# A hybrid decoder trunk on one core: weight slabs split earlier at the stages' seams, and six more convolution taps on TensorE

## The chip, the cores and the metric

One core of one Trainium2 chip runs the whole kernel. The metric is the device time in microseconds, the median of the runs. Before the change it is 932.27 us (three runs, 932.22 to 932.45).

## The reference

Two layers on 256 tokens of width 1024, all in float32. Each layer is an FFN, a token mixer and another FFN, and a final RMSNorm ends the trunk:

```python
for i in range(2):
    x = x + 0.5 * swiglu_ffn(rms_norm(x, ffn1_norm[i]), ffn1_w_in[i], ffn1_w_out[i])
    xn = rms_norm(x, mix_norm[i])
    x = x + (pool_conv_mixer(xn, ...) if i == 0 else sgu_mixer(xn, ...))
    x = x + 0.5 * swiglu_ffn(rms_norm(x, ffn2_norm[i]), ffn2_w_in[i], ffn2_w_out[i])
out = rms_norm(x, final_norm)
```

An FFN has hidden width 2816: `(silu(gate) * up) @ w_out` with gate and up from one input matrix of 1024 x 5632. The even mixer projects to 512 pooling channels and 2 x 512 convolution channels. The first go through causal means over 2, 4, 8 and 16 tokens, a 128 x 128 matrix for each group and a scale. The others go through `a * sigmoid(gate)`, a causal depthwise convolution of 31 taps, LayerNorm over the 512 channels, and swish. One output matrix joins both. The odd mixer is a spatial gating unit: GELU, LayerNorm, a masked 128 x 128 matrix for each of 8 heads along the tokens, and an output matrix.

## The kernel before

Every product with weights is computed in three fp32r matmuls (`three`, L960): both operands are split into a high and a low part, and hi x hi, hi x lo and lo x hi are summed. Weights come from HBM in slabs of 128 x 2048 floats. SyncE loads each slab in two halves into a ring of RAW = 3 buffers (`load`, L231); a load waits until the low part of the slab three before it is done. ScalarE copies a slab to its high part `w_hi` (`split`, L444). VectorE subtracts to get the low part `w_lo` (`split`, L660). Both parts stand in a ring of RING = 6 slabs, and a split waits until TensorE has used the slab six before it. On each of the two engines `split_to(n)` splits all slabs up to n that are still to be split, at the place where it stands. An engine works strictly in the order of the program, so these places decide what stands ahead of what.

There are six stages: 0 is FFN, 1 the even mixer, 2 and 3 are FFNs, 4 is the odd mixer and 5 an FFN. `b` is the first slab of a stage. An FFN has 11 units. A unit uses two input slabs (the upper and lower half of the 1024 input rows) for 256 gate and 256 up channels. Token tile 0 is summed in PSUM bank `ga`, token tile 1 in `ub`, 24 matmuls each. ScalarE applies silu to the gate half of a bank (`gate_rows`), and VectorE multiplies by the up half (`product_rows`, L753), which frees the bank for the next unit. The product is transposed by TensorE (`turned`, L1061) in the middle of the next unit. ScalarE copies its high part (`hidden_hi`), VectorE subtracts the low part (`hidden_lo`, L761), and then one output slab is used for the previous unit's hidden channels (`step_out`, L1126), summed in the `acc` banks. Units 1 to 8 run in a loop of two a turn (L529 on ScalarE, L794 on VectorE), each with three splits. A stage of this kind thus splits its slabs at four places: before the first gate, between the two first gates, before the loop and in the loop. The last two units have places of their own (L540, L819).

A stage ends with `tail` (L1089): token tile 0 is finished first, then tile 1, with the next norm's transposes for tile 0 inside it. VectorE adds the sum to the residual and scales it (`norm`, L692, lines 701 and 709), GpSimd takes the root.

In the even mixer the convolution is shared. Channel tile 3 (31 taps) and the last SHARED taps of channel tile 2 are computed on TensorE: ScalarE builds a diagonal matrix from a tap (`build_taps`, L561), sixteen of them standing at a time, and `convolve` (L1186) multiplies it by the shifted input in plain float32. All taps of tiles 0 and 1 and the first 31 - SHARED of tile 2 are multiply-adds on VectorE (`tap`, L837, line 846), with splits and the pooling's low parts between them. An add (L877) joins the two parts of tile 2, and then TensorE takes the mean over channels (L1227). The pooling needs window matrices, masked by GpSimd (`windows`, L386) as soon as VectorE has made the shares of the first tokens (`shares`, L769).

Of the kernel before, what the change touches and what calls it, by code (L numbers as in the profile page):

```python
# [31 lines left out]
def hybrid_trunk(nc, x, ffn1_norm, ffn1_w_in, ffn1_w_out, mix_norm, ffn2_norm, ffn2_w_in, ffn2_w_out,  # L32
# [51 lines left out]
    with ExitStack() as ctx:  # L84
# [67 lines left out]

        SHARED = 10
        pe_taps = [(CT - 1, q) for q in range(TAPS)] + [(CT - 2, q) for q in range(TAPS - SHARED, TAPS)]
        DIAGS = 2 * D // P

# [282 lines left out]
        def _(act):  # L441
            nxt = 0

            def split(n, i=None):  # L444


                act.wait_ge(raw_landed[n % RAW], at(32 * (n // RAW + 1), 32 * RING // RAW, i))
                if n >= RING:
                    act.wait_ge(slab_used, at(n - RING + 1, RING, i))
                o = 0  # L450
                if n == 0:
                    o = SLAB // 2
                    act.activation(w_hi[:, 0, 0:o], raw[:, 0, 0:o], ACT.Copy).then_inc(hi_half, 1)
                act.activation(w_hi[:, n % RING, o:], raw[:, n % RAW, o:], ACT.Copy).then_inc(hi_split, 1)  # L454

            def split_to(n):
                nonlocal nxt
                while nxt <= min(n, TOTAL - 1):
                    split(nxt)
                    nxt += 1  # L460
# [56 lines left out]
            for k, (kind, *_) in enumerate(stages):  # L517
                b, f = base[k], fill0[k]
                norm(k, 0)
                split_to(b)  # L520
                norm(k, 1)
                split_to(b + (2 if k == 0 else 1 if kind == "ffn" else 3))
                r, e = unit0[k], ffn0[k]
                if kind == "ffn":
                    gate_rows(0, b, r, f, ACT.Silu)
                    split_to(b + 3)
                    gate_rows(1, b, r, f, ACT.Silu)
                    split_to(b + 5)
                    with act.Fori(0, (STEPS - 3) // 2) as i:  # L529
                        for j in range(2):  # L530
                            n, s = b + 2 + 3 * j, 1 + j
                            hidden_hi(j, j, e + j, i)
                            split(n + 4, i)
                            gate_rows(0, n, r + s, f + s, ACT.Silu, i)
                            gate_rows(1, n, r + s, f + s, ACT.Silu, i)
                            split(n + 5, i)
                            split(n + 6, i)
                    nxt += 3 * (STEPS - 3)
                    n = b + 2 + 3 * (STEPS - 3)
                    for s in (STEPS - 2, STEPS - 1):  # L540
                        hidden_hi((s - 1) % 2, (s - 1) % 2, e + s - 1)
                        split_to(n + 5)
                        gate_rows(0, n, r + s, f + s, ACT.Silu)
                        gate_rows(1, n, r + s, f + s, ACT.Silu)
                        if s == STEPS - 1:
                            hidden_hi(2, 0, e + s)
                        split_to(n + 7)
                        n += 2
                elif kind == "mix0":
# [4 lines left out]
                    n = small[("hidden", k)]  # L554
# [6 lines left out]
                    def build_taps(lo, hi):  # L561
                        for m in range(lo, hi):
                            if m >= DIAGS:
                                act.wait_ge(tap_used, m - DIAGS + 1)
                            c, q = pe_taps[m]
                            act.activation(tap_diag(m), ident[:, :], ACT.Copy, scale=taps[:, c, q:q + 1])\
                                .then_inc(tap_built, 1)

                    gate(b + 2, f + 1, ACT.Sigmoid)
                    split_to(b + 6)  # L570
                    act.wait_ge(cols_ready, 1)
                    build_taps(0, DIAGS)

                    for t in range(TT):
                        if t == 0:
# [8 lines left out]
                    for j in range(2):  # L584
                        n = small[("pooled", j)]
# [68 lines left out]
        def _(dve):  # L654
# [17 lines left out]
            def split_to(n):  # L672
                nonlocal nxt
                while nxt <= min(n, TOTAL - 1):
                    split(nxt)
                    nxt += 1
# [71 lines left out]
            def product(n, f, out):  # L748
                dve.wait_ge(slab_used, n + 1)
                dve.wait_ge(ga_free, f + 1)  # L750
                dve.tensor_tensor(out, ub[:, :, :], sgh[:, 0, :, :], ALU.mult).then_inc(ub_free, 1)
# [28 lines left out]
            for k, (kind, *_) in enumerate(stages):  # L780
# [1 line left out]
                norm(k, 0)  # L782
                split_to(b)
                norm(k, 1)
                split_to(b + (2 if k == 0 else 1 if kind == "ffn" else 3))
                g = gated0[k]
                if kind == "ffn":
                    product_rows(0, g, e)
                    split_to(b + 3)
                    product_rows(1, g)  # L790
                    split_to(b + 5)
                    if k == 0:
                        shares()
                    with dve.Fori(0, (STEPS - 3) // 2) as i:  # L794
                        for j in range(2):
                            n, s = b + 2 + 3 * j, 1 + j
                            hidden_lo(j, j, e + j, i)
                            split(n + 4, i)
                            product_rows(0, g + 2 * s, e + s, i)
                            product_rows(1, g + 2 * s, e + s, i)  # L800
                            split(n + 5, i)
                            split(n + 6, i)
                    nxt += 3 * (STEPS - 3)
                    if k == 0:

                        n = small["taps"]
# [11 lines left out]
                    n = b + 2 + 3 * (STEPS - 3)  # L818
                    for s in (STEPS - 2, STEPS - 1):  # L819
                        hidden_lo((s - 1) % 2, (s - 1) % 2, e + s - 1)  # L820
                        split_to(n + 5)
                        product_rows(0, g + 2 * s, e + s)
                        product_rows(1, g + 2 * s)
                        if s == STEPS - 1:
                            hidden_lo(2, 0, e + s)
                        split_to(n + 7)
                        n += 2
                elif kind == "mix0":
# [26 lines left out]
                        tap(0)  # L855
                        tap(1)

                    split_to(b + 6)
                    product(b + 3, f + 1, conv_in[:, 2:4, LEAD:])
                    dve.wait_ge(ub_free, f + 2)  # L860
                    for q in range(5, TAPS):

                        for c in (0, 2, 1) if q - 5 < TAPS - SHARED else (0, 1):
                            tap(c)

                        if q in (12, 16):
                            split_to(b + 7 + (q - 12) // 4)
                        if q in (25, 27):
                            j = (q - 25) // 2
                            dve.wait_ge(mix_hi, j + 1)  # L870
                            dve.tensor_tensor(act_lo[:, 2 * j:2 * j + 2, :], mixed[:, 2 * j:2 * j + 2, :],
                                              act_hi[:, 2 * j:2 * j + 2, :].bitcast(F32), ALU.subtract)\
                                .then_inc(mix_ready, 1)
# [436 lines left out]
```

## Time and profile before

| | us |
|---|---|
| median of three runs | 932.27 |
| profiled execution | 932.27 |
| span of its trace | 930.5 |
| TensorE busy (matmuls) | 916.5 (98% of the span) |
| VectorE busy | 525.5 (56%) |
| ScalarE busy | 413.4 (44%) |
| GpSimd busy | 23.6 (3%) |

The granted clock of TensorE is full in all 40 slices of the span. The DMA engines move 183 GB/s on the mean, and they are busy for about half of the time. The chain that ended last is 88% TensorE and 7% VectorE. The three largest groups of VectorE and ScalarE are the low parts of slabs (349.0 us, 154 slabs), the high parts (289.2 us) and, far behind, the parts of the hidden tiles (30.4 and 26.3 us).

How to read it: matmuls overlap in the profile, so one of 128 x 512 shows 0.39 us while the next starts 0.23 us after it. Busy shares are means over stages with different limits. A wait in the view of waits is the idle time of an engine just before an instruction, with the engine and line that ended it.

### The profile page before, as it was taken

The page shows a single profiled execution, that of the slowest core. Times are in us where ns is not written, and L with a number is a line of the kernel's source. Part 1 is how long each engine was busy: PE and PEld are TensorE (multiplying, and loading weights), DVE is VectorE, ACT ScalarE, POOL GpSimd, SP SyncE. Part 2 cuts the span into 40 slices and gives each one's busy share as a digit, 9 for nine tenths or more (in the row PEclk, how much of TensorE's full clock was granted, in tenths as well). Part 3 has the DMA queues.
Part 4 walks back from the last instruction along what each step waited for, and adds up shares of the span by engine and source line. Part 5 has one row for each costly group of instructions (what it writes and reads, how often), then busy time and mean ns, then how long its engine had stood idle before and what let it go on. Part 6 is the DMA issues. An engine that isn't in the chain of part 4 may idle for free.

```text
span 930.5 us, 11397 instructions
## 1 busy us (share of the span) xinstructions
PE 916.5 (98%) x4349; PEld 764.2 (82%) x4349; DVE 525.5 (56%) x511; ACT 413.4 (44%) x452; POOL 23.6 (3%) x44
## 2 busy tenths in 40 slices
PE   8999999999999999999999999999999999999997
PEld 7888888879878888888878888888799888888885
DVE  5745455458976554453565554545678464454543
ACT  5544344446844442443444434424564263434432
POOL 1400000000000000000000000000000000000000
PEclk9999999999999999999999999999999999999999
DMA  8855646725313856476528465566284266455521
GB/s 279 295 185 181 225 145 206 259 92 189 105 46 118 289 178 207 157 255 240 182 91 267 152 205 190 180 217 213 90 304 149 91 221 231 155 207 180 181 113 46
DMA packets 126668, 170.20 MB, mean 183 GB/s; under 512 B 5237, under 2 KB 111241, under 8 KB 126632
## 3 DMA queue, kind: packets, MB, share of 16 engines
q1 hardware_dynamic: 126632, 169.70, 53.8%
q8 instruction: 25, 0.41, 0.2%
q14 instruction: 11, 0.09, 0.0%
HBM read 168.63 MB, written 1.05 MB: 182 GB/s over the span
## 4 chain that ended last, share of the span: by engine, by line
PE 88%; DVE 7%; ACT 2%; issue 1%; DMA 1%; POOL 0%; SPq 0%; POOLq 0%; ACTq 0%; DVEq 0%
PE ga L962 10%; PE ga L964 10%; PE ga L963 10%; PE ub L964 9%; PE ub L962 9%; PE ub L963 9%; PE acc L962 9%; PE acc L964 9%; PE acc L963 9%; DVE xs L846 3%; DVE w_lo L669 3%; PE tp L1066 2%; PE tp L1023 1%; ACT w_hi L454 1%; DMA raw<-in_ffn_w_in_dram 1%
## 5 line engine op out<-in xcount | busy, mean ns | idle before, releaser
L669 DVE TENSOR_TENSOR w_lo<-raw,w_hi 128x2048 fp32r<-128x2048 f32 (+1 forms) x154 | 349.0, 2290 | 116.2 <-ACT w_hi L454 115.6
L454 ACT ACTIVATE w_hi<-raw 128x2048 fp32r<-128x2048 f32 (+1 forms) x154 | 289.2, 1903 | 30.9 <-DMA raw<-in_ffn_w_in_dram 19.5
L962 PE MATMUL acc<-w_hi,act_hi 128*128 128x512 f32 x416 | 163.5, 393 | 0.0
L964 PE MATMUL acc<-w_hi,act_lo 128*128 128x512 f32 x416 | 162.0, 389 | 0.0
L963 PE MATMUL acc<-w_lo,act_hi 128*128 128x512 f32 x416 | 161.9, 389 | 0.0
L962 PE MATMUL ga<-w_hi,xn_hi 128*128 128x512 f32 x384 | 154.9, 403 | 0.4 <-DVE w_lo L669 0.3
L964 PE MATMUL ga<-w_hi,xn_lo 128*128 128x512 f32 x384 | 150.1, 391 | 0.0
L963 PE MATMUL ga<-w_lo,xn_hi 128*128 128x512 f32 x384 | 149.8, 390 | 0.0
L964 PE MATMUL ub<-w_hi,xn_lo 128*128 128x512 f32 x384 | 149.6, 390 | 0.0
L962 PE MATMUL ub<-w_hi,xn_hi 128*128 128x512 f32 x384 | 149.5, 389 | 0.0
L963 PE MATMUL ub<-w_lo,xn_hi 128*128 128x512 f32 x384 | 149.4, 389 | 0.0
L514 ACT ACTIVATE act_hi<-tp 128x512 fp32r<-128x512 f32 x44 | 26.3, 598 | 254.3 <-PE tp L1066 254.3
L764 DVE TENSOR_TENSOR act_lo<-tp,act_hi 128x512 fp32r<-128x512 f32 x44 | 30.4, 691 | 178.7 <-ACT act_hi L514 178.7
L964 PEld LDWEIGHTS acc<-w_hi,act_lo 128*128 128x128 f32 x416 | 78.1, 188 | 16.5
L963 PEld LDWEIGHTS acc<-w_lo,act_hi 128*128 128x128 f32 x416 | 78.1, 188 | 15.9
L962 PEld LDWEIGHTS acc<-w_hi,act_hi 128*128 128x128 f32 x416 | 78.1, 188 | 15.8
L964 PEld LDWEIGHTS ga<-w_hi,xn_lo 128*128 128x128 f32 x384 | 72.1, 188 | 15.8
L962 PEld LDWEIGHTS ub<-w_hi,xn_hi 128*128 128x128 f32 x384 | 72.1, 188 | 15.5 <-DVE xn_lo L716 0.3
L964 PEld LDWEIGHTS ub<-w_hi,xn_lo 128*128 128x128 f32 x384 | 72.1, 188 | 15.0
L962 PEld LDWEIGHTS ga<-w_hi,xn_hi 128*128 128x128 f32 x384 | 72.2, 188 | 14.7 <-DVE w_lo L669 1.2
L963 PEld LDWEIGHTS ub<-w_lo,xn_hi 128*128 128x128 f32 x384 | 72.1, 188 | 14.8
L963 PEld LDWEIGHTS ga<-w_lo,xn_hi 128*128 128x128 f32 x384 | 72.3, 188 | 13.4
(133 smaller groups left out, 585.7 us busy)
## 6 DMA issues: line engine op xcount, KB each, us to landing
raw<-in_ffn_w_in_dram SPq DMA_DIRECT2D x176, 512.0 KB, 4.8
raw<-in_ffn_w_out_dram SPq DMA_DIRECT2D x88, 512.0 KB, 4.0
raw<-in_sgu_w_in_dram SPq DMA_DIRECT2D x16, 512.0 KB, 4.5
raw<-in_ab_w_in_dram SPq DMA_DIRECT2D x12, 512.0 KB, 5.0
raw<-in_ab_w_out_dram SPq DMA_DIRECT2D x8, 512.0 KB, 3.9
raw<-in_sgu_w_out_dram SPq DMA_DIRECT2D x8, 512.0 KB, 5.4
gain<-in_ffn_norm_dram SPq DMA_DIRECT2D x4, 512.0 KB, 6.0
xres<-in_x_dram SPq DMA_DIRECT2D x2, 512.0 KB, 5.8
```

Of the source, the lines that this page charges most:

```text
L454: act.activation(w_hi[:, n % RING, o:], raw[:, n % RAW, o:], ACT.Copy).then_inc(hi_split, 1)
L514: act.activation(act_hi[:, 2 * slot:2 * slot + 2, :], tp[bank][:, :].rearrange("p (j t) -> p j t", j=2), ACT.Copy).then_inc(h_hi_done, 1)
L669: dve.tensor_tensor(w_lo[:, n % RING, o:], raw[:, n % RAW, o:], w_hi[:, n % RING, o:].bitcast(F32), ALU.subtract).then_inc(lo_split, 1)
L764: dve.tensor_tensor(act_lo[:, 2 * slot:2 * slot + 2, :], tp[bank][:, :].rearrange("p (j t) -> p j t", j=2), act_hi[:, 2 * slot:2 * slot + ...
L846: ins = dve.scalar_tensor_tensor(out=y[:, c, :], in0=conv_in[:, c, q:q + T], scalar=taps[:, c, q:q + 1], in1=y[:, c, :], op0=ALU.mult, op1 ...
L962: pe.matmul(dst, s_hi, m_hi, start=start, stop=False)
L963: pe.matmul(dst, s_hi, m_lo, start=False, stop=False)
L964: return pe.matmul(dst, s_lo, m_hi, start=False, stop=stop)
L1023: mm = pe.transpose(bank[:, c * P:(c + 1) * P], xs[:, t, o:o + P], ident[:, :])
L1066: mm = pe.transpose(bank[:, o:o + P], sgh[:, 1, t, j * P:(j + 1) * P], ident[:, :])
```

## The change

The convolution's share of TensorE in channel tile 2 grows from 10 taps to 16. In the FFN stages the splits move forward: before the first gate up to slab b+3 (before: b+2 in stage 0, b+1 in the others), between the gates up to b+4, before the loop up to b+7 (before b+5). In the loop each step splits slabs two further on. Of the two splits that stood behind the last hidden tile of a stage, one now stands before the last unit's gates. `shares` moves from before the loop to before the first product. In the even mixer ScalarE builds the first sixteen diagonals before it splits slab b+6. VectorE takes the second product before slabs b+5 and b+6, and splits b+6 after tap 8. The low parts of the pooling's result move from after taps 25 and 27 to after 19 and 21.

```diff
-        SHARED = 10
+        SHARED = 16
...
@@ ScalarE @@
-                split_to(b + (2 if k == 0 else 1 if kind == "ffn" else 3))
+                split_to(b + 3)
                 r, e = unit0[k], ffn0[k]
                 if kind == "ffn":
                     gate_rows(0, b, r, f, ACT.Silu)
-                    split_to(b + 3)
+                    split_to(b + 4)
                     gate_rows(1, b, r, f, ACT.Silu)
-                    split_to(b + 5)
+                    split_to(b + 7)
                     with act.Fori(0, (STEPS - 3) // 2) as i:
                         for j in range(2):
                             n, s = b + 2 + 3 * j, 1 + j
                             hidden_hi(j, j, e + j, i)
-                            split(n + 4, i)
+                            split(n + 6, i)
                             gate_rows(0, n, r + s, f + s, ACT.Silu, i)
                             gate_rows(1, n, r + s, f + s, ACT.Silu, i)
-                            split(n + 5, i)
-                            split(n + 6, i)
+                            split(n + 7, i)
+                            split(n + 8, i)
...
                         hidden_hi((s - 1) % 2, (s - 1) % 2, e + s - 1)
-                        split_to(n + 5)
+                        split_to(n + 6)
...
                     gate(b + 2, f + 1, ACT.Sigmoid)
-                    split_to(b + 6)
                     act.wait_ge(cols_ready, 1)
                     build_taps(0, DIAGS)
+                    split_to(b + 6)
...
@@ VectorE: the same moves of split and split_to around product_rows and hidden_lo, and @@
+                split_to(b + 3)
+                if k == 0:
+                    shares()
...
-                    split_to(b + 6)
                     product(b + 3, f + 1, conv_in[:, 2:4, LEAD:])
+                    split_to(b + 5)
                     dve.wait_ge(ub_free, f + 2)
                     for q in range(5, TAPS):
                         for c in (0, 2, 1) if q - 5 < TAPS - SHARED else (0, 1):
                             tap(c)
-                        if q in (12, 16):
-                            split_to(b + 7 + (q - 12) // 4)
-                        if q in (25, 27):
-                            j = (q - 25) // 2
+                        if q in (8, 12, 16):
+                            split_to(b + 6 + (q - 8) // 4)
+                        if q in (19, 21):
+                            j = (q - 19) // 2
```

## Rows read from the trace of the kernel before

**Rows 1.** Waits of TensorE: waited for, us in total, times, longest.

```profile
PE tp L1023 <- DVE xs L709: 4.8, 5, 1.2
```

**Rows 2.** Timeline of VectorE, end of stage 0: start us, us, line, operation, count.

```profile
192.21 4.50 DVE L669 TENSOR_TENSOR w_lo<-raw,w_hi 128x2048 fp32r<-128x2048 f32 x2 [1.11 <-ACT w_hi L454]
196.62 0.69 DVE L701 SCALAR_TENSOR_TENSOR xres<-acc,xres 128x512 f32<-128x512 f32 x1
```

**Rows 3.** Timeline of TensorE, end of stage 0; in brackets the idle time before.

```profile
194.85 0.39 PE L964 MATMUL acc<-w_hi,act_lo 128*128 128x512 f32 x1
...
198.93 0.39 PE L964 MATMUL acc<-w_hi,act_lo 128*128 128x512 f32 x1
200.49 1.29 PE L1023 MATMUL tp<-ident,xs 128*128 128x128 f32 x8 [1.18 <-DVE xs L709]
```

**Rows 4.** Timeline of TensorE, even mixer, from the taps to the mean.

```profile
255.83 3.62 PE L1191 MATMUL ub<-scratch,xs 128*128 128x256 f32 x16
...
262.23 0.39 PE L964 MATMUL acc<-w_hi,act_lo 128*128 128x512 f32 x1
263.38 1.97 PE L1227 MATMUL ub<-xs,avg 128*128 128x256 f32 x8 [0.76 <-DVE xs L877]
```

**Rows 5.** Timeline of VectorE, even mixer: two slabs, taps, the last add.

```profile
223.25 4.49 DVE L669 TENSOR_TENSOR w_lo<-raw,w_hi 128x2048 fp32r<-128x2048 f32 x2
...
229.10 8.80 DVE L846 SCALAR_TENSOR_TENSOR xs<-scratch,taps,xs 128x256 f32<-128x256 f32 x22
...
262.82 0.41 DVE L877 TENSOR_TENSOR xs<-ub,xs 128x256 f32<-128x256 f32 x1
```

**Rows 6.** Timeline of ScalarE, start of stage 2: the norm's last copy, two slabs.

```profile
293.96 0.60 ACT L477 ACTIVATE xn_hi<-tp 128x512 fp32r<-128x512 f32 x1 [0.53 <-PE tp L1023]
...
294.93 3.71 ACT L454 ACTIVATE w_hi<-raw 128x2048 fp32r<-128x2048 f32 x2
```

**Rows 7.** Timeline of VectorE, start of stage 2: the second product.

```profile
301.28 0.42 DVE L758 TENSOR_TENSOR sgh<-ub,sgh 128x256 f32<-128x256 f32 x1
```

**Rows 8.** Timeline of TensorE, stage 2: first matmuls of unit 1 and its output slab.

```profile
299.91 0.39 PE L962 MATMUL ga<-w_hi,xn_hi 128*128 128x512 f32 x1
...
311.29 0.39 PE L962 MATMUL acc<-w_hi,act_hi 128*128 128x512 f32 x1
```

**Rows 9.** Timeline of SyncE, stage 2: the issues of one slab's two halves.

```profile
304.66 0.82 SPq L237 DMA_DIRECT2D raw<-in_ffn_w_out_dram  x2
```

**Rows 10.** Landing of slabs b+5, b+6, b+7 of stage 2, two halves each.

```profile
DMA to landing us min/median/max: 3.8/4.3/4.8
...
DMA to landing us min/median/max: 4.9/5.4/5.9
...
DMA to landing us min/median/max: 4.4/4.8/5.2
```

**Rows 11.** Timeline of VectorE, stage 0: slabs 1 and 2, first share, first hidden tile.

```profile
17.91 4.48 DVE L669 TENSOR_TENSOR w_lo<-raw,w_hi 128x2048 fp32r<-128x2048 f32 x2
...
32.70 0.40 DVE L773 TENSOR_SCALAR share<-cnt_i 128x16 f32<-128x16 int32 x4
...
33.92 0.69 DVE L764 TENSOR_TENSOR act_lo<-tp,act_hi 128x512 fp32r<-128x512 f32 x1
```

**Rows 12.** Timeline of ScalarE, start of stage 5: table load and first gate.

```profile
744.02 1.28 ACT L509 ACT_TABLE_LOAD   x1
745.32 0.39 ACT L509 ACTIVATE sgh<-ga 128x256 f32<-128x256 f32 x1
```

**Rows 13.** Timeline of TensorE, stage 5: first matmul of unit 1.

```profile
749.88 0.50 PE L962 MATMUL ga<-w_hi,xn_hi 128*128 128x512 f32 x1 [0.33 <-DVE w_lo L669]
```

**Rows 14.** Timeline of TensorE, stage 0: first matmul of unit 1.

```profile
25.87 0.39 PE L962 MATMUL ga<-w_hi,xn_hi 128*128 128x512 f32 x1
```

**Rows 15.** Timeline of VectorE, stage 4: a slab while GpSimd masks the spatial weights.

```profile
686.60 3.08 DVE L669 TENSOR_TENSOR w_lo<-raw,w_hi 128x2048 fp32r<-128x2048 f32 x1 [1.49 <-ACT w_hi L454]
```

**Rows 16.** Timeline of ScalarE, start of stage 3: the norm's last copy.

```profile
482.23 0.60 ACT L477 ACTIVATE xn_hi<-tp 128x512 fp32r<-128x512 f32 x1 [0.53 <-PE tp L1023]
```

More of the change, by code:

```diff
@@ L784, in _ @@
                 norm(k, 1)
-                split_to(b + (2 if k == 0 else 1 if kind == "ffn" else 3))
+                split_to(b + 3)
+                if k == 0:
+                    shares()
                 g = gated0[k]
@@ L788, in _ @@
                     product_rows(0, g, e)
-                    split_to(b + 3)
+                    split_to(b + 4)
                     product_rows(1, g)
-                    split_to(b + 5)
-                    if k == 0:
-                        shares()
+                    split_to(b + 7)
                     with dve.Fori(0, (STEPS - 3) // 2) as i:
@@ L797, in _ @@
                             hidden_lo(j, j, e + j, i)
-                            split(n + 4, i)
+                            split(n + 6, i)
                             product_rows(0, g + 2 * s, e + s, i)
                             product_rows(1, g + 2 * s, e + s, i)
-                            split(n + 5, i)
-                            split(n + 6, i)
+                            split(n + 7, i)
+                            split(n + 8, i)
                     nxt += 3 * (STEPS - 3)
@@ L820, in _ @@
                         hidden_lo((s - 1) % 2, (s - 1) % 2, e + s - 1)
-                        split_to(n + 5)
+                        split_to(n + 6)
                         product_rows(0, g + 2 * s, e + s)
```

## The prediction

> **What bounds the kernel now.** I read the waits of TensorE first. Its largest entry is 4.8 us in the whole execution, in five waits for a norm's scaled rows before the transposes [rows 1]; the next inside the program is the 0.8 us before the LayerNorm mean of the even mixer [rows 4]. Inside the long loops of the FFN stages there is no entry for it at all. So the time is TensorE's instruction stream plus a few holes. The change can gain only holes that exist, or instructions that go; it loses every hole that it opens and every instruction that it adds. Splitting weight slabs earlier is worth nothing where TensorE does not wait for a slab. What has to be read is therefore each place where the order of ScalarE (w_hi) and VectorE (w_lo) changes: stage ends, stage starts, and the even mixer.
>
> **1. The ends of stages 0, 2 and 3 gain.** Before, VectorE subtracts two next-stage slabs there, 192.21 to 196.7, then the residual of token tile 0 starts at 196.62 (4.50 us for two, so 2.25 each, and residuals follow directly) [rows 2]. TensorE's last matmul of that tile started at 194.85 and took 0.39, so the sum was there at about 195.3 [rows 3]. After the change one of the two slabs is split before the last gates, where VectorE has room; the other ends at about 194.5, and the residual can start at 195.3, 1.3 us sooner. From the residual to the transposes it is 200.49 - 196.62 = 3.87 us, so they could start at 199.15. TensorE comes free at 198.93 + 0.23 = 199.16, 0.23 being the step from one such matmul to the next [rows 3]. The hole of 200.49 - 199.16 = 1.33 us closes, just. What is late next is nothing: both meet. The same pattern stands three times, in front of stages 1, 3 and 4 (five waits in rows 1; the other two belong to the first norm of the program). I take 1.25 us each: **-3.75 us** (bounds -4.0 and -3.4).
>
> **2. The even mixer loses.** Six more taps of channel tile 2 go from VectorE to TensorE. A tap is two records there, sixteen of them span 3.62 us with the drain of the last, and their starts are 3.45 us apart [rows 4]: 0.43 us a tap, 6 x 0.43 = 2.6 us, all of it on TensorE's stream. It buys the wait before the mean: 263.38 against 262.23 + 0.23 = 262.46 [rows 4], 0.9 us. TensorE would reach the mean at 262.46 + 2.6 = 265.06. Would VectorE be ready? Its taps cost 8.80 / 22 = 0.40 us, so six fewer save 2.4. On the other side, the product with the second gate now stands ahead of the two slabs that filled VectorE from 223.25 to 227.7 [rows 5]; it must wait for TensorE's bank, so up to 4.5 us of VectorE are lost in idling, and the slabs are done afterwards. The last add was at 262.82 [rows 5]; it comes between 260.4 and 264.9, and ends 0.41 later. Both bounds are at or below what TensorE needs, within 0.3. ScalarE builds six more diagonals in idle time, ahead of their use. So the mean moves from 263.38 to 265.06: **+1.7 us** (1.5 to 2.0). The moves of the pool split from taps 25 and 27 to 19 and 21 and of slab b+6 hide under the convolution and cost nothing.
>
> **3. The starts of the FFN stages lose most.** The products on VectorE free the two banks of gates; TensorE starts the second unit on them. The change puts slabs up to b+3 ahead of the first product, b+4 ahead of the second, and three slabs (b+5, b+6, b+7) instead of two ahead of the first hidden split.
>
> Stage 2, which enters with only slabs up to b+1 split. ScalarE ends the norm at 293.96 + 0.60 and can split two slabs at once, at 1.86 each (3.71 for two): 296.4 and 298.2 [rows 6]. VectorE: 298.6 and 300.85. The product of 0.42 [rows 7] ends at 301.25. TensorE starts the unit at 299.91 before [rows 8], so it waits **1.4 us**. The second product comes after b+4 (303.4) at 303.8, and TensorE wants that bank 12 matmuls, 2.7 us, after 301.3: free.
> Then the loads. The raw ring holds three slabs, so b+5, b+6, b+7 are issued when w_lo of b+2, b+3, b+4 is done: 298.6, 300.85, 303.4. The second half goes out about 0.4 later [rows 9], and the halves took up to 4.8, 5.9 and 5.2 us to land when these three slabs followed each other in this stage [rows 10]. With 0.1 for the hand-over they land at 303.9, 307.25 and 309.1. ScalarE: 305.8, 309.1, 311.0 (1.86 each). VectorE: 308.0, 311.4, 313.65. Only then the low half of the first hidden tile, 0.69 [rows 11], to 314.3. TensorE wants it 311.29 - 299.91 = 11.38 us after the start of the unit [rows 8], at 312.7: it waits **1.6 us** (0.3 if the loads land 1.3 sooner; 2.5 if they land 0.9 later). After that units have slack again: the last slab of a step is split in the 11 us before its next hidden tile.
>
> Stage 5 enters the same way, and its table load of 1.28 now comes behind two splits. Splits end at 745.85 and 747.7 on ScalarE, 748.1 and 750.35 on VectorE; the product at 750.75 against a unit that started at 749.88 [rows 12, 13]: **0.95 us**. Then the table load, the gate (0.39 [rows 12]) and slab b+4 to 751.2, w_lo 753.45, product 753.85, wanted at 753.5: **0.4 us**. Slab b+7 lands at 753.45 + 0.5 + 5.2 = 759.15 and is split to 761.0 and 763.2, the hidden tile at 763.9, wanted at 750.8 + 0.4 + 11.38 = 762.6: 1.3 us. The load queue of this stage is a little slower than that of stage 2, so I take **1.6 us** (0.3 to 2.3).
>
> Stage 0: w_lo of slab 2 ends at 17.91 + 4.48 = 22.4, slab 3 at 24.65, the pool shares (33.92 - 32.70 = 1.22) at 25.85 and the product at 26.25, wanted at 25.87 [rows 11, 14]: **0.45 us**. Slab 4 ends at 28.5, slab 7 lands at 34.2, is split to 36.1 and 38.3, hidden tile 39.0; wanted 26.3 + 11.38 = 37.7: 1.3 us. Fewer loads stand in line here, so **1.0 us** (0.2 to 2).
> The shares in front release GpSimd's window masks earlier, beside the first subtractions. A subtraction that ran while GpSimd masked the spatial weights took 3.08 us where 2.25 is usual [rows 15]; 0.8 us for one or two of them is in the upper end of this stage. By the Trainium skill ("SBUF — State Buffer", "Who interferes with whom") a tensor_tensor with both inputs in SBUF and a GpSimd instruction that reads SBUF exclude each other until the first is done, and the row agrees. If all three subtractions between the products and the hidden tile were met in that way, the stage would lose 2.4 us more and the forecast would be 940.4; the shares would then be the costliest move of the change.
>
> Stage 3 enters with b+2 split. One slab more: ScalarE from 482.8 [rows 16], w_lo at 486.9, product 487.3. The unit starts as far behind the norm as in stage 2 (299.91 - 293.96 = 5.95), at 488.2: free. b+7 is issued at 489.5, lands at 495.2, is split to 497.1 and 499.35, hidden tile at 500.0 against 499.6: **0.4 us** (0 to 1.2).
>
> Sum of the starts: 0.45 + 1.0 + 1.4 + 1.6 + 0.4 + 0.95 + 0.4 + 1.6 = **+7.8 us**. Mixer 1's start and the end of the program keep their order.
>
> **Sum.** -3.75 + 1.7 + 7.8 = +5.75 us. The profiled execution took 932.27 (span 930.5 and 1.8 around it), and the median of the runs is 932.27 as well, so the forecast is 938.0.
>
> **Rivals.**
> A. The loads land early enough and VectorE's third slab does not delay the hidden tile. Then only the bank waits stay: 0.45 + 1.4 + 0.95 + 0.4 = 3.2; with -3.75 and +1.7 it is +1.1, or 933.4, no difference that can be told. For it: the halves of the first of the three slabs landed in 3.8 and 4.8 us [rows 10]. Against it: three slabs back to back on VectorE alone are 6.75 us, and each of them needs a load issued only after the slab three before it.
> B. Faster. The place is the first product of stages 0, 2 and 5. Were the extra splits to run in idle time of both engines, as the same move does at the stage ends, all of part 3 would go, and -3.75 + 1.7 = -2.05 stays: 930.2. It decides from where w_lo of b+3 ends before TensorE has finished its first unit (299.9 in stage 2). For it: both engines stand idle for long stretches of a normal unit. Against it: TensorE's first unit takes 5.95 us from the norm's last copy, and two splits through both engines with the product take 7.3.
> C. The loads jam. Pulled together by the faster start, each lands about 1 us later than the three lines of [rows 10] say, stage 0 suffers from its small loads and from the masks, and the hidden waits become 2.0, 2.5, 1.2 and 2.3 instead of 4.6 in all. That is 3.4 more and 941.4.
> D. The stage ends gain nothing, since the residual is held by something else than the two slabs. Then 3.75 more, 941.8. The rows on both sides of 196.62 speak against it.
>
> **How the numbers follow.** Forecast 0.68, A 0.13, B 0.05, C 0.10, D 0.04. A run here can be told from no change at about 0.2%, 1.9 us, so from 934.1 up it is slower. The forecast's own range, with its hidden waits between half and one and a half, is 935.5 to 940.5; the range with part of A and C is 934.2 to 941.0. Slower: 0.68 + 0.10 + 0.04 and a little of A, 0.83. Same: 0.11. Faster: 0.06.
>
> **What would show it.** Part 1: no wait of TensorE before three of the norm transposes, residuals right after the last matmul of the tile. Part 2: 94 records of the tap line instead of 82, and no wait before the mean. Part 3: new waits of TensorE on ga for the product in stages 0, 2, 5 of 0.5 to 1.4 us, and on acc for act_lo of 1 to 2 us once in each of them. The forecast is wrong if these acc waits are missing, or if TensorE waits inside the loops.

## The result: 942.1 us, 1.0% slower

The changed kernel took 942.14 us at the median (941.78 to 942.53, 4 runs) against 932.36 for the one before. The ratio is 1.0104, with a 95% interval of 1.0087 to 1.0122. The profiled execution took 942.7 us, with a span of 940.9. The forecast was 938.0, slower, with a range up to 941.0: the sign was right, the size was not, and the time lies above the range.

### The profile page after: what moved, and what is told of

The parts are those of the page before. It is cut to its first block, busy times and chain, and to the rows that moved or that the text cites. A ratio compares the mean times of both kernels' runs of the same rounds, so it can differ in the third digit from the quotient of the medians.

```text
span 940.9 us, 11413 instructions
## 1 busy us (share of the span) xinstructions
PE 922.0 (98%) x4361; PEld 767.1 (82%) x4361; DVE 525.4 (56%) x505; ACT 418.8 (45%) x458; POOL 28.3 (3%) x44
## 4 chain that ended last, share of the span: by engine, by line
PE 87%; DMA 4%; DVE 3%; ACT 2%; issue 2%; SPq 0%; POOL 0%; POOLq 0%; DVEq 0%; ACTq 0%
PE acc L962 10%; PE acc L963 10%; PE acc L964 10%; PE ga L962 9%; PE ga L964 9%; PE ga L963 9%; PE ub L964 8%; PE ub L962 8%; PE ub L963 8%; DMA raw<-in_ffn_w_in_dram 2%; DVE w_lo L669 2%; PE tp L1066 2%; ACT w_hi L454 2%; DMA raw<-in_ffn_w_out_dram 2%; PE ga L1191 1%
## 5 line engine op out<-in xcount | busy, mean ns | idle before, releaser
L454 ACT ACTIVATE w_hi<-raw 128x2048 fp32r<-128x2048 f32 (+1 forms) x154 | 293.4, 1907 | 137.2 <-PE acc L964 97.1
L514 ACT ACTIVATE act_hi<-tp 128x512 fp32r<-128x512 f32 x44 | 26.2, 596 | 165.7 <-PE tp L1066 165.7
```

The source lines that it names most:

```text
L514: act.activation(act_hi[:, 2 * slot:2 * slot + 2, :], tp[bank][:, :].rearrange("p (j t) -> p j t", j=2), ACT.Copy).then_inc(h_hi_done, 1)
```

## The profile after, read against the one before

First the waits of TensorE in the changed kernel (waited for, us in total, times, longest). They answer to [rows 1].

```profile
PE acc L962 <- DVE act_lo L764: 5.2, 4, 2.3
PE ga L962 <- DVE sgh L758: 3.8, 4, 1.3
PE tp L1023 <- DVE xs L709: 1.5, 2, 1.1
PE ub L962 <- DVE sgh L758: 0.3, 1, 0.3
```

Three of the five waits for a norm's rows are gone, and the wait before the mean is gone. In their place stand four waits for the low part of a hidden tile and five for a product. Where they cost, the starts of the same instruction in both traces tell: TensorE hardly waits in between, so the difference of the starts changes only at a seam. The transposes (L1023 at a norm, L1066 in a unit) and the mean (L1227) serve as marks. These are timeline rows of TensorE before,

```profile
31.31 0.60 PE L1066 MATMUL tp<-ident,sgh 128*128 128x128 f32 x4
48.12 0.60 PE L1066 MATMUL tp<-ident,sgh 128*128 128x128 f32 x4
305.36 0.60 PE L1066 MATMUL tp<-ident,sgh 128*128 128x128 f32 x4
322.17 0.60 PE L1066 MATMUL tp<-ident,sgh 128*128 128x128 f32 x4
755.46 0.60 PE L1066 MATMUL tp<-ident,sgh 128*128 128x128 f32 x4
772.27 0.60 PE L1066 MATMUL tp<-ident,sgh 128*128 128x128 f32 x4
```

and the same marks after; 202.48 and 267.04 answer to [rows 3, 4]:

```profile
32.35 0.60 PE L1066 MATMUL tp<-ident,sgh 128*128 128x128 f32 x4
51.45 0.60 PE L1066 MATMUL tp<-ident,sgh 128*128 128x128 f32 x4
202.48 1.28 PE L1023 MATMUL tp<-ident,xs 128*128 128x128 f32 x8
267.04 1.89 PE L1227 MATMUL ub<-xs,avg 128*128 128x256 f32 x8
310.48 0.60 PE L1066 MATMUL tp<-ident,sgh 128*128 128x128 f32 x4
329.51 0.60 PE L1066 MATMUL tp<-ident,sgh 128*128 128x128 f32 x4
761.79 0.60 PE L1066 MATMUL tp<-ident,sgh 128*128 128x128 f32 x4
782.75 0.60 PE L1066 MATMUL tp<-ident,sgh 128*128 128x128 f32 x4
```

Taken at all 65 marks, the difference stands still within 0.1 us between the seams and moves as follows:

| seam | forecast, us | measured, us |
|---|---|---|
| start of stage 0 | +1.45 | +3.4 |
| ends of stages 0, 2 and 3 together | -3.75 | -4.0 (-1.33, -1.34, -1.35) |
| even mixer, up to the mean | +1.7 | +1.65 |
| start of stage 2 | +3.0 | +3.75 |
| start of stage 3 | +0.4 | +0.5 |
| start of stage 5 | +2.95 | +5.35 |
| sum (with -0.1 between the seams) | +5.75 | +10.5 |

This ledger is that of the profiled execution, which took 942.7; the median lies 0.6 us below it. Behind their first turn the loops add nothing. The error of 4.7 us lies in the starts of stages 0, 2 and 5. The timeline of TensorE at the start of stage 5 shows both waits, and something that was in no part of the forecast:

```profile
755.92 0.47 PE L962 MATMUL ga<-w_hi,xn_hi 128*128 128x512 f32 x1 [1.26 <-DVE sgh L758]
...
770.17 0.47 PE L962 MATMUL acc<-w_hi,act_hi 128*128 128x512 f32 x1 [2.28 <-DVE act_lo L764]
...
770.70 0.40 PE L964 MATMUL acc<-w_hi,act_lo 128*128 128x512 f32 x1
770.94 0.59 PE L962 MATMUL acc<-w_hi,act_hi 128*128 128x512 f32 x1
771.33 0.63 PE L963 MATMUL acc<-w_lo,act_hi 128*128 128x512 f32 x1
...
774.58 0.39 PE L962 MATMUL acc<-w_hi,act_hi 128*128 128x512 f32 x1
```

From 0.8 us behind the wait of 2.28 us on, the matmuls stretch from 0.39 to 0.63, and their starts stand 0.43 apart instead of 0.23. By 774.58 it is over. The view by windows gives the granted clock (the third column from the right, after the busy times; the last two are the DMA share and GB/s):

```profile
766.00:770.00 4.00, 1.89 (x9) 1.23 (x7) 2.94 (x3) 2.18 (x3) 0.00 (x0) 1.00 1.00 321
770.00:775.00 5.00, 4.83 (x14) 3.87 (x15) 3.68 (x5) 3.77 (x4) 0.00 (x0) 0.66 0.71 271
```

TensorE fell to the lower of its two levels, 1.2 GHz, right behind the wait. The matmul at 770.17 stood at 761.39 before. Against the mark at 761.79 (755.46 before) it has lost 2.45 us, which is the wait, and up to the next mark another 1.7 us are lost, which are the slow matmuls. By the Trainium skill ("TensorE: Matmul & The Clock Gate", "Part 1: The HAM clock gate") the throttled clock is the default state and activity releases it; that the clock fell behind a standstill agrees with that much. In the kernel before no wait behind the program's first 2 us was longer than 1.2 us [rows 1], and none of its matmuls behind the start is stretched.

## The experiments

Each was run beside the kernel before, whose median was 932.26 to 932.35 in these runs.

**mix_only.** The edits of the even mixer alone.

```diff
-        SHARED = 10
+        SHARED = 16
@@ and the three moves of the even mixer in the diff of the change @@
```

> Only the even mixer's edits (16 shared taps, order of slabs and products there). Theory: TensorE's stream grows by 6 taps x 0.43 = 2.6 us and the wait of 0.9 before the mean goes, so +1.7 us, 934.0; the mean's first matmul moves from 263.4 to about 265.1. Rival 1 (VectorE's idling before the product makes it late for the mean): +2.5 and more, with a wait on the last add. Rival 2 (the taps run in time that TensorE has left): 931.4 to 932.4.

Measured 933.77 us (ratio 1.0015, 1.0005 to 1.0025). The mean starts here, where it stood at 263.38 [rows 4]:

```profile
264.91 1.89 PE L1227 MATMUL ub<-xs,avg 128*128 128x256 f32 x8
```

and VectorE's last add ends at 263.90 + 0.42 = 264.32, so it is in time:

```profile
263.90 0.42 DVE L877 TENSOR_TENSOR xs<-ub,xs 128x256 f32<-128x256 f32 x1
```

The first theory holds; both rivals fall. Taps went to the engine that bounds the kernel, and the 0.9 us wait they bought off was cheaper than they are.

**ends_only.** One slab moved ahead of the last unit's gates, nothing else.

```diff
-                        split_to(n + 5)
+                        split_to(n + 5 + (s == STEPS - 1))
```

> Only one slab moved ahead of the last unit's gates in every FFN; starts, loop and mixer as before. Theory: the three holes of 1.33 us before the norm transposes close and nothing is lost, -4.0 us, 928.3. Rival (the gain at the ends needs the deeper order of the loop, or the loads): no change, 932.3.

Measured 928.13 us (0.9953, 0.9936 to 0.9970), and 928.16 in a second set of runs. Its marks move by -1.35, -1.34 and -1.37 at the three ends and nowhere else. The whole gain of the change is in this line, and needs none of the rest.

**bank_only.** The first two places of the change in front of the FFN loops, with the depth of the kernel before.

```diff
-                split_to(b + (2 if k == 0 else 1 if kind == "ffn" else 3))
+                split_to(b + 3)
@@ between gate_rows(0) and gate_rows(1), and between the products @@
-                    split_to(b + 3)
+                    split_to(b + 4)
```

> Only the two splits in front of the first product and between the first products; loop depth, mixer and shares as before. Theory: TensorE waits for the first product in stage 2 (1.5 us) and stage 5 (0.9, and 0.3 for the second bank), not in stages 0 and 3, and never on act_lo: +2.7 us, 935.1. Rival (the loads are what is late, whatever the order): waits on act_lo of about 2 us as well, 938 to 940.

Measured 936.2 us (1.0041, 1.0027 to 1.0055), +3.9. There is no wait on act_lo, so the rival falls:

```profile
PE ga L962 <- DVE sgh L758: 2.5, 2, 1.3
PE ub L962 <- DVE sgh L758: 0.8, 1, 0.8
```

Stages 2 and 5 lose 1.6 and 1.2 us, as worked out. The miss is stage 0, where its mark moves by 1.06: the second product stands behind slab 4, whose load is not there in time. The pool shares stand at their old place here, so these 1.06 us need no shares.

**hidden_only.** The depth of the change, with the first two places of the kernel before, so that one slab more than in the change stands in front of the first hidden tile.

```diff
@@ against the kernel before, on ScalarE and VectorE alike @@
-                    split_to(b + 5)
+                    split_to(b + 7)
@@ in the loop @@
-                            split(n + 4, i)
+                            split(n + 6, i)
...
-                            split(n + 5, i)
-                            split(n + 6, i)
+                            split(n + 7, i)
+                            split(n + 8, i)
```

> Only the depth: slabs up to b+7 ahead of the first hidden tile and two further on in the loop, and the slab moved at the ends; the first two places, shares and mixer as before, so that four slabs instead of three stand ahead of the first hidden tile. Theory: no wait for a product in stages 2 and 5, but TensorE waits 3 to 4 us for act_lo once in every FFN stage, with the clock at its lower level for some matmuls behind it; with -4.0 at the ends 941 to 948. Rival (the third slab on VectorE does not delay the tile): 928.3.

Measured 953.7 us (1.0222, 1.0205 to 1.0239), more than any theory said. TensorE waits in each of the four stages:

```profile
42.74 0.76 PE L962 MATMUL acc<-w_hi,act_hi 128*128 128x512 f32 x1 [5.36 <-DVE act_lo L764]
321.96 0.76 PE L962 MATMUL acc<-w_hi,act_hi 128*128 128x512 f32 x1 [3.90 <-DVE act_lo L764]
514.76 0.47 PE L962 MATMUL acc<-w_hi,act_hi 128*128 128x512 f32 x1 [2.93 <-DVE act_lo L764]
781.99 0.77 PE L962 MATMUL acc<-w_hi,act_hi 128*128 128x512 f32 x1 [4.90 <-DVE act_lo L764]
```

The four starts lose 8.0, 6.8, 4.7 and 6.7 us, 26.2 in all, of which 17.1 are the waits. 38 matmuls are stretched to 0.6 us and more; at 0.2 us each they are some 8 of the 9 that are left. So these four waits cost half as much again as the view of waits says. The order of the theory is right, its size was too small.

**hid_first.** The change, but slab b+7 behind the first hidden tile (the loop's first turn written out). It takes the place of slab b+8 there, and b+8 moves behind the gates of unit 1.

```diff
-                    split_to(b + 7)
+                    split_to(b + 6)
+                    for j in range(2):
+                        n, s = b + 2 + 3 * j, 1 + j
+                        hidden_hi(j, j, e + j)
+                        split_to(n + 5 + j)
+                        gate_rows(0, n, r + s, f + s, ACT.Silu)
+                        gate_rows(1, n, r + s, f + s, ACT.Silu)
+                        split_to(n + 8)
@@ VectorE alike; the loop starts at 1 @@
```

> The changed kernel, but slab b+7 is split behind the first hidden tile on both engines; everything else as changed. Theory (VectorE's order is what delays the tile): the waits on act_lo of 0.6, 2.0, 0.3 and 2.3 us go, and the low clock behind the last of them with them: 942.1 - 7 = 935. Rival (the loads are late in any order): b+7 or b+8 then stands ahead of the gates of unit 1 and the same time is lost in a wait for a product: 940 to 942.

Measured 933.9 us (1.0018, 1.0008 to 1.0027): 8.2 us less than the changed kernel, for two slabs one place further back. No wait on act_lo is left, nor the one for the second unit's product in stage 0. VectorE at the start of stage 2, where L676 is the low part of a slab and L771 that of the hidden tile:

```profile
311.00 2.29 DVE L676 TENSOR_TENSOR w_lo<-raw,w_hi 128x2048 fp32r<-128x2048 f32 x1 [1.45 <-ACT w_hi L454]
313.21 0.68 DVE L771 TENSOR_TENSOR act_lo<-tp,act_hi 128x512 fp32r<-128x512 f32 x1
313.81 2.28 DVE L676 TENSOR_TENSOR w_lo<-raw,w_hi 128x2048 fp32r<-128x2048 f32 x1
```

The same slab subtracted behind the tile costs nothing, and the gates behind it are in time. The loads come no sooner (the third slab of stage 2 takes 6.5 us from its last issue to landing, 6.1 in the changed kernel); it is the order that made their lateness count.

**small_late.** The change, with the seven small loads of the even mixer issued behind the loads of the loop.

```diff
-                    if k == 0:
-                        sp.dma_start(pw, ...)      # and six more
                     with sp.Fori(1, (STEPS - 3) // 2) as i:
                         turn(i, i)
+                    if k == 0:
+                        sp.dma_start(pw, ...)      # and six more
```

> The changed kernel with the seven small loads of the even mixer issued behind the loads of the loop in stage 0. Theory: slab 8 is no longer 8 us on its way, the wait of 1.1 us for the second unit's product goes: -1.4 us, 940.7, and the wait on act_lo stays. Rival (slab 8 is late because it is issued late): 942.1.

The median, 943.36 (939.69 to 945.44), says nothing, since the runs lie 5.7 us apart. The trace does: the marks of stage 0 are 32.32 and 49.90, so the second step is 49.90 - 32.32 = 17.58 instead of 51.45 - 32.35 = 19.10, and the wait of 1.09 us for the second unit's product is not there. Slab 8 lands 4.7 us after its last issue here and 7.4 us in the changed kernel. The 1.5 us were predicted. Stages 2 and 5 have longer waits (2.26 and 2.83 us) in this execution, which takes it back.

**shares_back.** The change, with the pool shares again in front of the loop.

```diff
-                if k == 0:
-                    shares()
...
                     split_to(b + 7)
+                    if k == 0:
+                        shares()
```

> The changed kernel with the pool shares back in front of the loop. Theory: the first product of stage 0 is no longer late by the 1.2 us of the shares, its wait of 0.2 to 0.3 us goes; the wait for the second bank stays, as it is slab 4's landing that makes it: 941.5 to 942.0. Rival (GpSimd's masks, released early, slow the subtractions): they meet other subtractions now, 940.5 or less.

Measured 945.52 us (943.96 to 947.14), which neither theory said. The time alone tells little: the changed kernel itself took 945.89 in a later set of runs (below). The trace tells more. The first product is in time, but the second now waits 0.75 us instead of 0.27, and the first mark of the stage moves by 1.04 us, as it did in the change. And with the third slab in front of the loop the shares stand between that slab and the hidden tile:

```profile
36.34 2.29 DVE L669 TENSOR_TENSOR w_lo<-raw,w_hi 128x2048 fp32r<-128x2048 f32 x1 [0.85 <-ACT w_hi L454]
38.55 0.40 DVE L773 TENSOR_SCALAR share<-cnt_i 128x16 f32<-128x16 int32 x4
...
39.77 0.69 DVE L764 TENSOR_TENSOR act_lo<-tp,act_hi 128x512 fp32r<-128x512 f32 x1
```

The wait for the tile is 2.04 us there, and eight stretched matmuls follow. From 38.55 to 39.77, 1.2 us of VectorE between the slab and the tile are the shares. So going back gained nothing in front and put 1.2 us in the way of the tile. That it costs the whole kernel time is not shown, since the changed kernel's own wait for this tile was 0.64 us in one trace and 2.06 in another.

**ramp.** The kernel before, with the loop depth of the change reached in the two units of a written-out first turn.

```diff
@@ first turn, written out, ScalarE and VectorE alike @@
+                        split_to(n + 4 + j)     # ahead of the gates
+                        split_to(n + 7 + j)     # behind them
@@ in the loop: n + 6, n + 7, n + 8; in the last units split_to(n + 6) @@
```

> The kernel before with the loop's greater depth, but reached step by step: starts as before, one more slab in each of the first two units behind their gates, then the changed loop and ends; mixer and shares as before. Theory: depth itself costs nothing, only what stands ahead of a late consumer does: as the kernel with the ends alone, 928.1 to 928.5. Rival (a deeper order makes loads or gates late in the loop): 930 or more, with waits of TensorE in unit 2.

Measured 928.41 us (0.9958, 0.9942 to 0.9975), as ends_only. Depth itself costs nothing and gains nothing.

**filler, filler_25, after_again.** The change with 8 unused matmuls in front of the wait for the hidden tile, in stage 5 alone and in stages 2 and 5, and the changed kernel once more beside the latter.

```diff
                         slab_ready(n, i)
+                        if start and k in (2, 5):       # filler: k == 5
+                            for _ in range(8):
+                                pe.matmul(tp[1][:, 0:P], ones[:, :], avg[:, :], start=True, stop=True)
                         pe.wait_ge(h_done, at(done, 2, i))
```

> The changed kernel with 8 unused float32 matmuls (1.9 us) of TensorE in stage 5 where it waits 2.3 us for act_lo; their result is not read. Theory: the wait itself stays, but the clock does not fall behind it, so the nine matmuls that took 0.43 us each take 0.23 again: -1.7 us where it fell, about 940.5. Rival (the clock falls for another reason, or the loss is caught up by a later wait): 942.1.

> The changed kernel with 8 unused float32 matmuls (1.9 us) in stage 2 and in stage 5 where TensorE waits for act_lo. Theory: with no long standstill the clock falls in neither stage; the median is the ledger without it, 942.7 - 1.7 - 0.2 = 940.5 to 941, and the runs lie within 0.5 us of each other. Rival (the falls have nothing to do with the waits): 942 to 944 with a spread of 1.5 us, as with filler in stage 5 alone.

> The changed kernel once more. Theory: runs with no fall, one or two of them differ by 1.7 to 2.2 us each, so 940.5 to 944.5 between them. Rival (one fixed loss): all within 0.5 us of 942.1.

Medians: filler 943.85 (942.70 to 944.07), filler_25 944.54 (943.17 to 945.44), after_again 945.89 (943.47 to 946.36). The times that were expected of the fillers did not come, and the changed kernel itself was 3.8 us slower than in its first runs. The rival "all within 0.5 us of 942.1" falls, and three of the four runs lie above the theory's range of 940.5 to 944.5. filler_25 lies 1.35 us below after_again, its partner, but their runs overlap. What the traces say is told by the waits. In after_again they were

```profile
40.45 0.47 PE L962 MATMUL acc<-w_hi,act_hi 128*128 128x512 f32 x1 [2.06 <-DVE act_lo L764]
318.83 0.47 PE L962 MATMUL acc<-w_hi,act_hi 128*128 128x512 f32 x1 [2.28 <-DVE act_lo L764]
...
773.13 0.60 PE L962 MATMUL acc<-w_hi,act_hi 128*128 128x512 f32 x1 [2.52 <-DVE act_lo L764]
```

and in filler_25, where those of stages 2 and 5 are what the filler leaves of them (stage 3 is left out in both: 1.03 and 1.52 us),

```profile
40.37 0.47 PE L962 MATMUL acc<-w_hi,act_hi 128*128 128x512 f32 x1 [2.04 <-DVE act_lo L764]
320.28 0.50 PE L962 MATMUL acc<-w_hi,act_hi 128*128 128x512 f32 x1 [0.34 <-DVE act_lo L764]
...
773.50 0.50 PE L962 MATMUL acc<-w_hi,act_hi 128*128 128x512 f32 x1 [0.72 <-DVE act_lo L764]
```

None of the three starts with a filler has a stretched matmul (stage 5 in filler, stages 2 and 5 in filler_25). Between the marks, the start of stage 5 loses 2.0 and 2.8 us with filler against 4.1 and 4.4 in the changed kernel's two traces. Falls came only where no filler stood: in filler in stage 2, as in after_again, and in filler_25 in stage 0. This speaks for the standstill as the cause of the fall, since work without use in its place went with no fall in three of three starts. It is not proof: three of the twelve long waits without a filler had no fall either. That a filler lowers the whole time is not shown: what is spared in one stage was lost to longer waits and a fall in another.

**ends_b8.** Beyond the change: ends_only, and slab b+8 of the mixer behind the last add.

```diff
-                        if q in (12, 16):
-                            split_to(b + 7 + (q - 12) // 4)
+                        if q == 12:
+                            split_to(b + 7)
...
                     dve.tensor_tensor(y[:, 2, :], ub[:, 1, :], y[:, 2, :], ALU.add).then_inc(conv_step, 1)
+                    split_to(b + 8)
```

> The kernel with the ends alone, and in the even mixer slab b+8 split behind the last add on VectorE instead of among the taps (ten taps shared as before). Theory: VectorE reaches the last add 2.2 us sooner, the wait of 0.8 us before the mean goes, and the slab is split while VectorE waits for the mean: 928.1 - 0.9 = 927.2. Rival (the load that waits for that slab is late at the next stage's start): 928.1 or more.

Measured 927.26 us (0.9945, 0.9931 to 0.9958), with ends_only at 928.16 on the same chip. The wait before the mean is gone without a single tap moved to TensorE, and the slab runs where VectorE waited 2.15 us for the mean. Of these kernels it is the fastest.

```profile
259.36 0.42 DVE L877 TENSOR_TENSOR xs<-ub,xs 128x256 f32<-128x256 f32 x1
259.69 2.28 DVE L669 TENSOR_TENSOR w_lo<-raw,w_hi 128x2048 fp32r<-128x2048 f32 x1
263.12 1.29 DVE L883 TENSOR_TENSOR xs<-xs,ub 128x512 f32<-128x512 f32 x2 [1.15 <-PE ub L1228]
```

## Why the prediction was wrong in size

The steps that failed are terms of part 3. The waits for the hidden tile were too small in stages 2 and 5 (1.6 us each; 2.2 and 2.45 measured), since the third slab's load was given 5.2 us and took 6.1 and 6.2. Three terms were put at nothing: the second bank of stage 0 (0.6 measured), the second unit of stage 0, by the sentence "After that units have slack again" (1.5), and TensorE's clock behind a wait (1.7 in the profiled execution).

**Part 1, the ends.** Right: -4.0 us for the -3.75 of the text, shown alone by ends_only (-4.1). After the change the residual waits for TensorE and not for a slab: it starts at 198.60 in stage 0, and the transposes follow the matmul stream without a hole.

**Part 2, the mixer.** Right: +1.65 in the ledger and +1.5 alone for the +1.7 of the text. VectorE was late by less than its bounds allowed, and not binding.

**Part 3, the bank waits.** Right in stages 2 and 5: between the marks of the norm and the first matmul of the unit, 1.5 and 0.9 us for the 1.4 and 0.95 of the text, and by the starts 0.3 us for the second bank of stage 5 for 0.4. In stage 0 they were 1.1 us for 0.45: the second product stands behind slab 4, which landed at about 24.8, and I had taken it to be there. The first product was late by 0.4 us behind the shares, as worked out, but that cost nothing of its own: bank_only and shares_back, with no shares in front, lose the same 1.06 and 1.04 us.

**Part 3, the hidden tile.** The mechanism is right, and hid_first shows it: 8.2 us, with the second unit of stage 0 and the clock in them, hang on the places of slabs b+7 and b+8. The sizes failed. The text let slab b+7 land 5.2 us after its second half was issued, the latency of stage 2 in one trace of the kernel before. The three slabs of stage 2, whose rows before are [rows 10]:

```profile
DMA to landing us min/median/max: 3.7/4.2/4.8
...
DMA to landing us min/median/max: 4.8/5.3/5.8
...
DMA to landing us min/median/max: 5.2/5.7/6.1
```

The third took 6.1 us and not 5.2. The wait was 2.2 us by the starts for the 1.6 of the text. Up to b+6 every landing of this stage came within 0.1 us of the text, once the 3.6 us that the kernel is behind are taken off; b+7 came 0.8 us late. In stage 5 the third took 6.2 us as well, and the wait was 2.45 us for 1.6. There it could have been read beforehand, for the third slab of stage 5 in the kernel before shows

```profile
DMA to landing us min/median/max: 5.3/5.7/6.2
```

With 6.2 in place of 5.2 the text's 1.3 us for this stage would have been 2.3. Of rival C, which got 0.10, this is a part only: it had every one of the three loads about 1 us late and the four hidden waits at 8.0 us together; they were about 6.0 by the starts, for 4.6 in the text.

**"After that units have slack again".** False in stage 0, and a wait of TensorE inside the loop's first turn was one of the text's own signs of being wrong. Slab 8 is split ahead of the gates of unit 1, and it was late by its small loads and by the backlog:

```profile
41.16 1.92 ACT L454 ACTIVATE w_hi<-raw 128x2048 fp32r<-128x2048 f32 x1 [4.81 <-DMA raw<-in_ffn_w_in_dram]
```

ScalarE stood 4.8 us for it with both gates behind it, and TensorE waited 1.09 us for the product. small_late takes the wait away. That is 1.5 us that the text did not have.

**The clock.** No step spoke of it. It is 1.7 us in the profiled execution. It is no fixed part of the time: the mean granted clock was 0.997 there and 0.999, 0.998, 0.997 and 0.999 in the four other runs (941.78, 942.18, 942.53 and 942.11), where the kernel before has 0.998 to 0.999. So two of the four runs show no sign of a fall, and even they lie above the range. Their waits are not on record.

**The sum of the miss.** Stage 5 has 2.4 too little: 0.85 for the load and 1.7 for the clock, less 0.1 for a bank. Stage 2 has 0.75, of which the hidden tile is 0.6. Stage 0 has 1.9: 0.6 for the banks, 1.5 for the second unit, less 0.2 for the tile. Stage 3 has 0.1. Together 5.15, and the ends, the mixer and the stretches between give 0.4 back: the 4.7 us.

**GpSimd's masks.** A subtraction beside them took 2.51 and one 2.43 us instead of 2.29, which is 0.4 us in all; in the kernel before one beside them took 2.57. With the rule of the Trainium skill ("SBUF — State Buffer", "Who interferes with whom") the prediction had weighed 2.4 us; the measurement decides, and the shares' move is a small term. The exclusion itself is in the trace, with the loss on the other side. GpSimd's first two masks after the change, and VectorE's subtraction beside them,

```profile
25.78 3.77 POOL L393 TENSOR_SCALAR_AFFINE_SELECT scratch<-scratch 128x1024 f32<-128x1024 f32 x2 [11.86 <-DVE scratch L778]
26.77 2.29 DVE L669 TENSOR_TENSOR w_lo<-raw,w_hi 128x2048 fp32r<-128x2048 f32 x1 [0.73 <-ACT w_hi L454]
```

and the same two masks before, with no slab's subtraction beside them:

```profile
33.99 1.65 POOL L393 TENSOR_SCALAR_AFFINE_SELECT scratch<-scratch 128x1024 f32<-128x1024 f32 x2 [20.03 <-DVE scratch L778]
```

The masks took 2.1 us longer (GpSimd's spans are rough in the profile) and the subtraction its usual 2.29. Here it was the mask that stood, and no wait of TensorE ends with it.

**Left open.** Why the waits for the hidden tile lay at 0.64 us in stage 0 in one execution and at 2.06 in another, and why the changed kernel's median moved from 942.1 to 945.9 between two sets of runs, while the kernel before stayed at 932.3. The second set ran on chip 2; the chip of the first is not on record, and on chip 8 the variants filler and small_late took 943.85 and 943.36, so a part of the chip is neither shown nor excluded. The landing of the loads is what differs in front of the waits, but no run held it fixed.

## What to carry to other kernels

When a prefetch is made deeper, depth is not what costs; what costs is each extra piece placed ahead of a consumer that is due, and a ring that is full makes every piece wait for a load issued only just before. Put the extra pieces behind the due consumer, one each step. And price a new wait of the bounding engine with what follows it: behind the wait of 2.28 us its clock fell and added another 1.7.

## What the runs showed of the hardware

In the traces of the changed kernel and its variants, hidden_only left out, there are 12 waits of 1.96 to 2.83 us for a hidden tile. Behind 9 of them six to eight matmuls ran at the lower clock, behind 3 (1.96, 2.06 and 2.83 us) none. Behind the 11 waits of up to 1.52 us (two of them shortened by a filler), and behind every wait of the kernel before from the first norm on, there is none. The fall in the changed kernel's first trace cost 1.7 us.

How long the third of three 1 MB slabs takes to land (from its last issue) varies from one execution to the next, and in stage 2 it went with how closely they were asked for: where 4.7 us lay between the first and the third, 6.1 to 6.7 us in all eight traces; where it was 5.5 us, 4.9 to 5.3 us in five traces and 6.6 and 6.7 us in two. The forecast rested on one of the five [rows 10]. In stage 5 it was 5.4 to 6.8 us at 4.7 and at 5.3 us alike.

Where a subtraction of VectorE with both inputs in SBUF and a mask of GpSimd met, it was now the one and now the other that stood: the subtraction took 3.08 us instead of 2.29 beside one long mask [rows 15], and two masks took 3.77 us instead of 1.65 beside one subtraction.
